# Copying the two expert tables into one: 32 copies of 4 MB from GpSimd's queue, or 128 pieces of 1 MB, most of them on the weights' queue

## The reference

```python
mod_x = silu(c) @ w_mod + b_mod                    # six shifts, scales and gates; the same for the context
px = modulate(rms_norm(x), sh1, sc1) @ w_in        # q, k, v | hq, zf, zb, i, g
na_x = neighbourhood_attention(q, k, v, k_ctx, v_ctx, rpb)
hg_x = hgrn2_mixer(...)                            # two gated recurrences, forward and backward in time
x = x + gt1 * (concat(na_x, hg_x) @ w_out)
x = x + gt2 * peer_ffn(modulate(rms_norm(x), sh2, sc2), wq, keys, u, v)
```

```python
a = gelu(einsum('tpkd,td->tpk', u[idx], t)); out = einsum('tpk,tpkd->td', g * a, v[idx])
```

## Time and profile before

| | |
|---|---|
| median of 3 runs | 3895.64 us (3894.32 to 3897.06) |
| the profiled execution | 3882.41 us |
| its span in the trace | 3880.6 us |
| PE busy | 3198.9 us (82%) |
| DVE busy | 2138.6 us (55%) |
| POOL busy | 691.3 us (18%) |
| copies of the tables | 32 of 4096 KB |
| HBM written | 136.31 MB |

### The profile page before, as it was taken

How to read it: one execution, slowest core, us unless ns; L and a number is a source line. 1 busy time by engine, 2 the same in 40 slices (tenths; PEclk the granted TensorE clock), 3 DMA queues, 4 the chain that set the end, 5 groups by cost and what they waited for, 6 DMA issues and landing times. The chain is left out here.

```text
span 3880.6 us, 34820 instructions
## 1 busy us (share of the span) xinstructions
PE 3198.9 (82%) x12170; PEld 2142.1 (55%) x12170; DVE 2138.6 (55%) x3672; ACT 890.6 (23%) x2174; POOL 691.3 (18%) x655
## 2 busy tenths in 40 slices
PE   6499888788777777777777789778999899779998
PEld 6388677666222222322222267366887686458876
DVE  2122368656776774685444462346774434767753
ACT  2011333122222222222222220151220102312201
POOL 0000234101444343443343320000000000000000
PEclk6699888899999999999999999579999998889999
DMA  9999852125999999999999822001332230013322
GB/s 356 298 337 350 266 180 82 60 66 196 421 421 422 417 417 421 416 410 421 418 419 422 373 84 87 0 1 60 98 97 87 86 99 28 1 49 98 97 87 71
DMA packets 152752, 845.71 MB, mean 218 GB/s; under 512 B 13793, under 2 KB 14049, under 8 KB 86049
## 3 DMA queue, kind: packets, MB, share of 16 engines
q0 software_dynamic: 107968, 678.73, 44.8%
q1 hardware_dynamic: 44640, 165.12, 13.5%
HBM read 841.70 MB, written 136.31 MB: 252 GB/s over the span
## 5 line engine op out<-in xcount | busy, mean ns | idle before, releaser
L721 PE MATMUL PS<-AR,HC 128*128 128x512 f32 x1536 | 726.7, 618 | 249.0 <-ACT HC L1138 247.4
L192 PE MATMUL PS<-AR_r,RHI 128*128 128x512 f32 x1888 | 767.9, 407 | 182.9 <-DVE AR_r L1307 94.3
L194 PE MATMUL PS<-AR_r,RING_r 128*128 128x512 f32 x1888 | 746.7, 396 | 0.0
L1492 DVE SCALAR_TENSOR_TENSOR AR<-AR 128x1024 f32<-128x1024 f32 x384 | 470.2, 1225 | 359.7 <-DMA AR<-peer_uv,XC 356.9
L721 PEld LDWEIGHTS PS<-AR,HC 128*128 128x128 f32 x1536 | 283.5, 194 | 691.3 <-ACT HC L1138 393.2
L193 PE MATMUL PS<-AR_r,RHI 128*128 128x512 f32 x1504 | 594.8, 395 | 0.0
L445 POOL DMA_INDIRECT AR<-peer_uv,XC x384 | 398.7, 1038 | 739.8 <-PE PS L721 545.0
L192 PEld LDWEIGHTS PS<-AR_r,RHI 128*128 128x128 f32 x1888 | 361.8, 192 | 292.8 <-issue 89.7
L1289 DVE CAST RHI<-RING 128x1024 fp32r<-128x1024 f32 x256 | 178.6, 698 | 582.7 <-DMA RING<-in_wstream 519.3
L194 PEld LDWEIGHTS PS<-AR_r,RING_r 128*128 128x128 f32 x1888 | 362.2, 192 | 77.4
L193 PEld LDWEIGHTS PS<-AR_r,RHI 128*128 128x128 f32 x1504 | 288.6, 192 | 62.6 <-issue 6.0
(11 more groups left out here) (314 smaller groups left out, 3677.8 us busy)
## 6 DMA issues: line engine op xcount, KB each, us to landing
RING<-in_wstream SPq DMA_DIRECT2D x304, 512.0 KB, 3.6
peer_uv<-in_peer_u POOLq DMA_DIRECT2D x16, 4096.0 KB, 80.6
peer_uv<-in_peer_v POOLq DMA_DIRECT2D x16, 4096.0 KB, 83.5
AR<-peer_uv,XC POOLq DMA_INDIRECT x384, 13.6
XL<-in_xl SPq DMA_DIRECT2D x1, 2048.0 KB, 9.9
RHI_f<-peer_uv,XC POOLq DMA_INDIRECT x128, 13.6
AR<-in_strips POOLq DMA_DIRECT2D x1, 2048.0 KB, 10.3
out_x<-XL SPq DMA_DIRECT2D x1, 2048.0 KB, 6.3
```

The costliest lines, as they stand in the source:

```text
L192: pe.matmul(out, sh, mh, start=start, stop=False)
L194: return pe.matmul(out, sl, mh, start=False, stop=stop)
L721: mm = pe.matmul(bank(2 * (tt % 2) + x), DIAG[:, n % NDIAG, :], ROWS_UV[n % NROW][:, D + 512 * x:D + 512 * x + 512], start=(j == 0), stop= ...
L1492: dve.scalar_tensor_tensor(JUNK[n % 2], ROWS_UV[n % NROW][:, 0:D], 1.0, HT[:, n // SLOTS, :], ALU.mult, ALU.mult, accum_out=RAW[:, n:n + 1 ...
```

## The change

The copies are cut into 128 pieces of 1 MB (256 rows of one table, piece i copies `peer_u` for even i and `peer_v` for odd i). SP issues 96 of them on its own queue, one right behind each of the 88 weight chunks from q to wq, and a second behind the 8 chunks of mod2 and mod3 whose number is a multiple of 4. GpSimd issues the other 32, one ahead of each bias tile of the attention. GpSimd's copies ahead of barriers 1 and 2 are gone, with its wait for the inputs. No copy waits for an older one any more; the gathers wait for two totals.

```diff
-COPY_ROWS = 1024
+COPY_ROWS = 256
 COPIES = 2 * NKEYS * NKEYS // COPY_ROWS
-COPIES_AHEAD = 8
+COPIES_AFTER, _n = {}, 0
+for _c in range(FIRST["q"], FIRST["rq"]):
+    _more = 2 if FIRST["mod2"] <= _c < FIRST["out"] and _c % 4 == 0 else 1
+    COPIES_AFTER[_c] = range(_n, _n + _more)
+    _n += _more
...
+        def copy_rows(eng, i, done):
+            rows, x = slice(COPY_ROWS * (i // 2), COPY_ROWS * (i // 2 + 1)), i % 2
+            eng.dma_start(PEER_UV[rows, D * x:D * x + D], t[("peer_u", "peer_v")[x]][rows]).then_inc(done, 16)
...
-            for j in range(NSLOT):
-                sp.dma_start(RING[:, j, :], t["wstream"][j]).then_inc(w_landed[j], 16)
-            with sp.Fori(1, NCHUNK // NSLOT) as g:
+            for c in range(FIRST["rq"]):
+                if c >= NSLOT:
+                    sp.wait_ge(chunk_used, c - NSLOT + 1)
+                sp.dma_start(RING[:, c % NSLOT, :], t["wstream"][c]).then_inc(w_landed[c % NSLOT], 16)
+                for i in COPIES_AFTER.get(c, ()):
+                    copy_rows(sp, i, uv_copied)
+            with sp.Fori(FIRST["rq"] // NSLOT, NCHUNK // NSLOT) as g:
...
-            pool.wait_ge(s_in, 80)
-            copy_rows(9)
             barrier(pool, 1)
-            copy_rows(15)
             barrier(pool, 2)
             pool.dma_start(XCF, t["level_masks"]).then_inc(s_hm, 16)
...
-                if i % 4 == 0:
-                    copy_rows(1)
+                copy_rows(pool, COPIES - 1 - i, uv_copied_late)
...
-            for j in range(COPIES_AHEAD):
-                pool.wait_ge(uv_copied[j], 16 * (COPIES // COPIES_AHEAD))
+            pool.wait_ge(uv_copied, 16 * (COPIES - NA_HEADS * NCB))
+            pool.wait_ge(uv_copied_late, 16 * NA_HEADS * NCB)
```

More of the change, by code:

```diff
@@ L11 @@
-import itertools
 from contextlib import ExitStack
@@ L69 @@
     NCHUNK += _n
+COPIES_AFTER, _n = {}, 0
[3 more added lines that the diff above has]
+    _n += _more
+assert _n + NA_HEADS * NCB == COPIES
 WHOLE = [(FIRST[_name], dict(SECTIONS)[_name]) for _name in ("mod1", "mod2", "mod3")]
@@ L335, in build @@
         pk_s, pk_sc, pk_top, pk_exp, pk_idx = (sem(f"pk_{k}") for k in ("s", "sc", "top", "exp", "idx"))
-        uv_copied = [sem(f"peer_uv_copied{j}") for j in range(COPIES_AHEAD)]
+        uv_copied, uv_copied_late = sem("peer_uv_copied"), sem("peer_uv_copied_late")
         row_landed = [sem(f"row_landed{j}") for j in range(NROW)]
```

## The result

The changed kernel takes 3821.7 us (median of 4 runs, 3820.9 to 3829.8), the kernel before in the same comparison 3895.0. The ratio is 0.9819 (95% interval 0.9802 to 0.9836): 73 us less, where 67 were forecast. The profiled execution took 3821.8 us with a span of 3820.0. Against the span of before that is only 60.6 us.

A forecast was written before the change was run, and what follows sets the result against it. GpSimd's drains at the barriers were taken to wait for its open table copies. Gains of 60.7 and 11.8 less a loss of 5.5 gave 67.0 us: 3895.6 - 67.0 = 3828.6 us, range 3806 to 3852.

The forecast's parts named there:

- mod1, gain 3.1: First modulation, 0 to 93 us: PE's wait for a chunk sharing the engines with copies goes, gain 3.1 us.
- Barrier 1, 55.0 and 2.6: Barrier 1 waits for VectorE alone: PE's gap goes, 55.0 us, and its cold matmuls after it, 2.6 us.
- Projections, 0: q to g: pieces on the weights' queue stay hidden under PE, 4.9 against 5.44 us, so 0.
- Barrier 2, 11.8: Barrier 2 falls at about 395.9 with only the bias table open, gain 11.8 us; masks issued 72.5 us sooner.
- Attention, loss 5.5: GpSimd's copies still set the attention's end; SP's leftover transfers add 5.5 us; barrier 3 near 462, wait about 16 us.
- the second case of the prediction: Rival, 20%: pieces at 3.2 us or less fit in PE's 108 us of attention; total 3810 to 3814.
- Recurrences, 0 with 2 us to spare: Modulation chunks 52 to 79 carry 35 pieces; chunk 53 lands at about 15, wanted at 17.2; cost 0.
- out and wq, 0: One piece a tile, at most 1.5 us of lateness inside the slack, so 0.
- the 0.2% that I named as what a measurement tells: Claim that a measurement here tells 0.2%, 8 us, from no change.
- The price of a piece: Unknown cost of a 1 MB HBM-to-HBM piece, above all on SP's queue; taken as 3.6 us.
- The sign that I named as making the prediction wrong: Pieces on SP's queue running at another rate than on GpSimd's would make the prediction wrong.
- The case of an unoverlapped fixed part: Rival, 5%: each DMA's 2.35 us paid in full, a piece 6.0 us; some 3900, or 3970 with SP's queue.

The follow-up runs named there:

- the second profiles: Kernel before and changed kernel each run again without an edit: before 3884.7 us, changed 3824.0 us (ratio 0.9850).
- the size-only run: Kernel before with each 4 MB copy cut into four 1 MB pieces, same places and drains: 3896.3 us, ratio 1.0061.

## Why the prediction was right, step by step

The total was right, and its reason: GpSimd's drains wait for its copies. The term that carried it, taken over from the gap at barrier 1, holds with a remark that the prediction lacked. The attention's term was right with a wrong price of a piece in it.

1. *mod1, gain 3.1.* PE's first q matmul came at 89.37 instead of 93.17: 3.8. In the second profiles it was 92.74 instead of 94.89: 2.2.
2. *Barrier 1, 55.0 and 2.6.* With mod1, 60.7 were forecast; the fourth q tile was evacuated at 114.32 where it had been 175.80: 61.5. But to treat it as a cost of its own was right only because the copies behind it were moved as well: with that drain alone removed, 12.6 us came.
3. *Projections, 0.* Right: PE waited for no chunk from q to g. Missed was a loss of 2.7 us at the first g tile. The idle time of 3.13 us ahead of it stands in both traces; in the first profile of before, the window behind it was granted 1.00, and here 0.50 (the second profiles of both kernels show 0.57 and 0.50, so this loss is not the change's):

```profile
312.00:314.00 2.00, 2.00 (x6) 1.53 (x5) 1.83 (x2) 0.73 (x1) 0.00 (x0) 0.50 0.92 377
```

4. *Barrier 2, 11.8.* The masks went out at 337.23, 70.5 us sooner where 72.5 were forecast: 61.5 - 2.7 + 11.7. Right to 0.1 for the step itself.
5. *Attention, loss 5.5.* From the masks to barrier 3 it took 127.5 us, 6.4 more than before, and barrier 3 fell at 464.7 (462 forecast). PE's gap was 12.5 and not 16, since PE itself ended at 452.2 and not at 446: it started 1.7 us later, and its clock fell about 2 us after the 3.1 us gap and came back at 365, so the first blocks ran at 1.2 GHz for 23 us, where they had for 15 before. That loss was hidden under the copies. The term itself came out of two errors. Its own numbers give 23 - 16.3 = 6.7 us left over from SP, not 5.5. And a piece did not cost 3.6 us. GpSimd's first, 31st and last piece were issued at 337.8, 433.5 and 436.6:

```profile
peer_uv<-in_peer_v POOLq DMA_DIRECT2D x1, 1024.0 KB, 17.8
...
peer_uv<-in_peer_v POOLq DMA_DIRECT2D x1, 1024.0 KB, 21.2
...
peer_uv<-in_peer_u POOLq DMA_DIRECT2D x1, 1024.0 KB, 26.7
```

```profile
442.00:444.00 2.00, 2.00 (x12) 1.36 (x11) 0.60 (x2) 0.12 (x1) 0.00 (x0) 1.00 0.99 313
452.00:454.00 2.00, 0.24 (x3) 0.00 (x0) 0.29 (x1) 0.00 (x0) 0.00 (x0) 1.00 0.54 213
460.00:462.00 2.00, 0.00 (x0) 0.00 (x0) 0.00 (x0) 0.00 (x0) 0.00 (x0) 0.50 0.16 68
```

By the count of their semaphore the first landed at 355.6 and the 31st at 454.6, 3.3 us apart on average (99.0 / 30). The last was complete 8.7 us after the 31st, while the DMA share fell from 0.99 to 0.16: most of the 16 engines were done long before the slowest. At 3.3 us the 32 pieces are 106 us, which fits into PE's 108, so by the second case of the prediction the attention should have ended with PE. It did not: the pieces go out at PE's pace with some six open, and the drain waits for the slowest engine's part of the last one. A price too high by 0.3 us a piece and a tail that the prediction did not have came to nearly the same sum, which is luck.
6. *Recurrences, 0 with 2 us to spare.* The sixth chunk, named there as the hard place, was late by 1.1 us here and 1.8 in the second profile. The step's estimate was some 3 us short; to the first gather the whole part lost 1.9 us.
7. *out and wq, 0.* Right: PE waited for no chunk there. Eight pieces more in wq already cost 4 us.

Forecast for the first gather was 867, measured 872.4: 62.2 us gained instead of 67. Of the missing 5, 2.7 are the clock ahead of g, 0.9 the attention and 1.9 the recurrences, less the 0.8 more at the start. The 2.7 us of the clock are not the change's. The median lies 6.9 us below its forecast (3821.7 against 3828.6) and the profiled execution 6.4 above its own (3821.8 against 3815.4), since the median of before and its profiled execution, from which the two are counted, differ by 13; single profiles cannot split that further. So the steps can be judged to a few us and the total to about 7, and the 0.2% that I named as what a measurement tells is too fine: on the same chip before ran from 3862 to 3904.

**The price of a piece** was taken as 3.6 us. In the size-only run it is 2 to 6% over a quarter of a copy, in the attention of the changed kernel 3.3 us with a tail of 8.7 behind the last. The sign that I named as making the prediction wrong, another rate on SP's queue, did not show. From 360 to 440 us the changed kernel moves GpSimd's pieces, and the kernel with the late pieces on SP moves SP's:

```profile
360.00:440.00 80.00, 79.43 (x438) 57.93 (x438) 52.06 (x97) 30.42 (x72) 33.36 (x49) 0.97 1.01 316
...
360.00:440.00 80.00, 79.96 (x462) 58.67 (x461) 41.05 (x105) 33.02 (x79) 17.87 (x24) 1.00 1.00 311
```

The case of an unoverlapped fixed part, the fall to 3900 and beyond, is excluded. The Trainium skill ("DMA: Bandwidth & Descriptors", Anatomy of one DMA) gives 2.0 us a DMA beside its bytes. The size-only run shows at most 0.3 us for each of the 27 DMAs that it adds ahead of barrier 1 (8.6 us later in all). There other pieces are open behind each one, which is the likely reason and was not tested by itself.

**What the change is made of.** Removing three drains, and moving nothing, gives 0.9815; the change gives 0.9819 on its chip and 0.9850 on another. Cutting the copies costs 0.6% where GpSimd issues them, and pays only on the weights' queue, where 4 MB ahead of a chunk cost 6 to 10 us in single profiles. The 12.5 to 19 us at barrier 3 are left on the table by the last 8 pieces of GpSimd.

## What to carry to other kernels

A barrier that drains GpSimd also waits for the DMAs which GpSimd has open (drains of the other engines with copies open were not run), so long background copies belong on a queue whose engine takes part in no drain, or the barrier should be signalled without one. Several gaps at successive drains can be one backlog: test by removing one of them before adding them up. On a queue shared with loads that somebody waits for, keep each background piece shorter than the cover of the loads behind it, and look for the place where these loads are used back to back.

## What was not expected of the hardware

TensorE's clock did not return at the same point of the same work: in the differential attention 2.4 GHz came back between 1040 and 1070 us after the last gather, 16 us of the total. After the same idle time of 3.13 us it had fallen in one execution (0.50) and not in another (1.00). The clock also moves what looks like a matter of DMAs: of the 8.0 us by which a weight chunk was later without the drain (9.1 against 1.1), 4.4 are PE at the higher clock wanting it sooner, and 3.6 the chunk landing later beside a piece of GpSimd's. And the last of a row of pieces was complete 8.7 us after the one before it, where those ahead of it came 3.3 us apart.
